# Third half tile ahead of a norm, and block making shared out anew between ScalarE and VectorE

## The reference, cut to what matters

```python
def _rmsnorm(x, g):
    y = x32 * lax.rsqrt(jnp.mean(x32 * x32, axis=-1, keepdims=True) + EPS)
    return (y * g.astype(jnp.float32)).astype(x.dtype)
def _modulate(h, shift, scale):
    return h * (1 + scale[:, None, :]) + shift[:, None, :]
...
    mod = cond @ ada_w[layer] + ada_b[layer]
    h = _modulate(_rmsnorm(x, norm1_g[layer]), sh1, sc1)
    y = _pool_mixer(...)                       # layer 0; layer 1: _dilated_attention
    hkv = _modulate(_rmsnorm(x, kv_norm_g), kv_shift, kv_scale)   # layer 1: a second activation
    kv = hkv @ w_kv
    x = x + g1[:, None, :] * y
    h = _modulate(_rmsnorm(x, norm2_g[layer]), sh2, sc2)
    x = x + g2[:, None, :] * _conv_ffn(h, w_up, conv_w, conv_b, w_down)
```

## Time and profile before

| | us |
|---|---|
| median of 3 runs | 2740.91 |
| lowest, highest | 2738.64, 2741.95 |
| the profiled execution | 2740.4 |
| its span | 2738.6 |
| PE busy in it | 2668.8 |
| DVE, ACT, POOL busy | 1391.9, 1034.7, 110.1 |

### The profile page before, as it was taken

One profiled execution on the slowest core, in us unless ns is written; L12 is line 12 of the kernel. 1 busy time (PEld: TensorE's weight loads), 2 busy tenths in 40 slices (PEclk: granted clock), 3 DMA queues, 4 the chain that ended last, 5 costly groups with the idle time before them and its releaser, 6 DMA issues.

```text
span 2738.6 us, 32934 instructions
## 1 busy us (share of the span) xinstructions
PE 2668.8 (97%) x13810; PEld 2148.9 (78%) x13810; DVE 1391.9 (51%) x2147; ACT 1034.7 (38%) x1525; POOL 110.1 (4%) x87
## 2 busy tenths in 40 slices
PE   7989999999999999999999999999999999999998
PEld 3578888877777777888888777788888777788887
DVE  6767767544444445543445654543444554543343
ACT  2243233453333334532343554422233555432232
POOL 0000000000000000000000110010010110010010
PEclk9989999999999999999999999999999999999999
DMA  7445645322222121223223121223223121223232
GB/s 299 185 161 207 247 180 204 116 82 78 78 78 72 68 78 62 78 98 110 93 94 121 50 81 55 101 94 105 92 97 118 62 77 62 92 93 115 78 104 74
DMA packets 46850, 297.03 MB, mean 108 GB/s; under 512 B 5104, under 2 KB 7280, under 8 KB 17520
## 3 DMA queue, kind: packets, MB, share of 16 engines
q1 hardware_dynamic: 46560, 294.42, 29.5%
q10 hardware_dynamic: 144, 0.52, 0.1%
HBM read 292.82 MB, written 2.10 MB: 108 GB/s over the span
## 4 chain that ended last, share of the span: by engine, by line
PE 90%; ACT 2%; DVE 2%; issue 0%; DVEq 0%
PE PS L506 88%; PE PS L564 1%; DVE WL L1414 1%; ACT H1H L972 0%; ACT WH L972 0%; DVE AR L1437 0%; DVE XT L1417 0%; DVE AA L1414 0%; ACT H2Hb L972 0%; ACT V0b L972 0%; ACT V1b L972 0%; DVE H1L L1414 0%; ACT AA L972 0%; ACT V2b L972 0%; ACT OC L972 0%
## 5 line engine op out<-in xcount | busy, mean ns | idle before, releaser
L506 PE MATMUL PS<-H1H,WH 128*128 128x512 f32 (+1 forms) x2256 | 885.8, 393 | 20.3 <-DVE WL L1414 12.6
L506 PE MATMUL PS<-H1H,WL 128*128 128x512 f32 (+1 forms) x2256 | 865.5, 384 | 0.0
L506 PE MATMUL PS<-H1L,WH 128*128 128x512 f32 (+1 forms) x2256 | 864.8, 383 | 0.0
L1414 DVE TENSOR_TENSOR WL<-RAW,WH 128x1024 fp32r<-128x1024 f32 (+1 forms) x400 | 526.8, 1318 | 461.3 <-ACT WH L972 460.7
L972 ACT ACTIVATE WH<-RAW 128x1024 fp32r<-128x1024 f32 (+1 forms) x400 | 439.7, 1101 | 270.0 <-PE PS L506 242.8
L506 PEld LDWEIGHTS PS<-H1H,WH 128*128 128x128 f32 x2256 | 427.6, 190 | 114.0 <-DVE WL L1414 16.7
L506 PEld LDWEIGHTS PS<-H1L,WH 128*128 128x128 f32 x2256 | 427.8, 190 | 84.3 <-issue 5.5
L506 PEld LDWEIGHTS PS<-H1H,WL 128*128 128x128 f32 x2256 | 427.1, 189 | 83.0
L506 PE MATMUL PS<-H2Hb,WH 128*128 128x512 f32 (+1 forms) x408 | 162.5, 398 | 4.0 <-issue 3.0
L506 PE MATMUL PS<-H2Hb,WL 128*128 128x512 f32 (+1 forms) x408 | 155.1, 380 | 0.0
L506 PE MATMUL PS<-H2Lb,WH 128*128 128x512 f32 (+1 forms) x408 | 154.8, 380 | 0.0
(11 more groups left out here) (252 smaller groups left out, 3085.0 us busy)
## 6 DMA issues: line engine op xcount, KB each, us to landing
RAW<-stream SPq DMA_DIRECT2D x170, 1024.0 KB, 4.8
AR<-stream SPq DMA_DIRECT2D x56, 1024.0 KB, 6.9
RAW<-stream SPq DMA_DIRECT2D x64, 704.0 KB, 4.0
...
```

The source lines that it names most:

```text
L506: return nc.tensor.matmul(out, weights, moving, start=start, stop=stop, skip_group_check=True)
L1414: return nc.vector.tensor_tensor(out, a, b, op)
```

## The change

- `HALVED` gives a number of half tiles for each norm: three for norms 1 to 3, still two for the last. Tiles 14, 74 and 154 are now multiplied in halves as well. `SQN`, `SUMN`, `RES`, `nth` and `added` count accordingly. Part 0's norm stands four blocks into the first half 1, in a bank of its own.
- `banks` writes out the banks of the half tiles and of the next three tiles by hand.
- The plain block V is made by DVE (`shifted`, a `tensor_scalar` with two operations) instead of ACT; DVE runs divide, shifted and low one, two and three blocks behind each other, and residuals, sums and preps stand between them. ACT makes the high block only.
- At edge 2 ACT makes each block of the second activation's high part after that block's second high half of the first; the plain blocks follow, in six buffers instead of three.
- `entry` takes four blocks of x = 0, then four of x = 1, then the norm of part 1, then the rest.
- The prep of the last tile of the projection and one iteration of the loops ahead move into the edge. At edge 1 three modulations in a row stand ahead of it.
- At the end `final_g_2` is multiplied into x by ACT ahead of DVE's last step, which becomes a `tensor_tensor`.

The diff, cut to its core:

```diff
-HALVED = (1, 2, 3, 8)
-
-RES = {"pool": 0, FFN0: 10, WO0: 28, FFN1: 38, OUT0: 54, FFN2: 62, OUT1: 78, FFN3: 86}
+HALVED = {1: 3, 2: 3, 3: 3, 8: 2}
+
+RES = {"pool": 0, FFN0: 11, WO0: 30, FFN1: 41, OUT0: 57, FFN2: 65, OUT1: 81, FFN3: 89}
...
-    for t in range(FFN0, ATT0 - 2):
+    place(halves(14, 1, "norm1") + list(range(FFN0, FFN0 + 3)), (0, 1, 2, 3, 4, 5, 7, 6, 0, 1))
+    for t in range(FFN0 + 3, ATT0 - 3):
         take(t)
-    halves(ATT0 - 2, "norm2")
-    for t in range(ATT0, ATT0 + 3):
-        take(t, (2, 3, 4))
+    place(halves(ATT0 - 3, 2, "norm2") + list(range(ATT0, ATT0 + 3)), (5, 6, 0, 1, 5, 6, 7, 2, 3, 4))
...
         for part in range(2):
-            for x in range(2):
+            for x in range(m):
                 b = BANK[t + x, part]
                 q.wait_ge(*c.low(t + x))
                 vacate(b)
                 for k in order:
-                    if (part, x, k) == (1, 0, order[n // 2]):
+                    if (part, x, k) == (1, 0, order[4]):
                         half_norm(v, bank, 0)
...
-        for k in range(8):
-            if k == 4:
-                half_norm(v, bank, 1)
-            for x in range(2):
+        for x in range(2):
+            for k in range(4):
                 some(x, 0, k)
-        for k in range(8):
-            some(2, 0, k)
+        half_norm(v, bank, 1)
+        for x, blocks in ((0, (4,)), (1, (4,)), (2, range(5))):
+            for k in blocks:
+                some(x, 0, k)
+        for k in range(5, 8):
+            for x in range(3):
+                some(x, 0, k)
         for k in range(4):
             for x in range(3):
...
-            kw = {"scale": c.AB[:, gains + k:gains + k + 1], "bias": c.mod(shift + k, 1)}
-            q.wait_ge(c.nt, 8 + n + e + 1)
-            act(part_of(c.H1H, k, part), T, ACT.Identity, **kw)
-            q.wait_ge(c.nld, n + e - 3 if e > 3 else n)
-            act(c.NORM[v]["V"][e % 4][:, 0:256], T, ACT.Identity, **kw).then_inc(c.nv, 1)
+            q.wait_ge(c.nt, 8 + 16 * a - 16 + e + 1)
+            act(part_of(c.H1H, k, part), c.NORM[v]["T"][e % 3][:, 0:256], ACT.Identity,
+                scale=c.AB[:, gains + k:gains + k + 1], bias=c.mod(shift + k, 1)).then_inc(c.nh, 1)
         return make
 
     def edge(v, bank, first, t0, out, make):
 
+        prep(t0 - 1)
+        for k in (5, 6, 7):
+            half_square(v, k, 0, first)
+        half_root(v, bank, out, 0)
+        make(0, 0)
+        half_square(v, 5, 1, first)
+        make(0, 1)
         prep(t0)
-        half_square(v, 6, 0, first)
-        half_square(v, 7, 0, first)
-        half_root(v, bank, out, 0)
+        make(0, 2)
+        make(0, 3)
         half_square(v, 6, 1, first)
+        make(0, 4)
         prep(t0 + 1)
-        for k in range(4):
-            make(0, k)
+        make(0, 5)
         half_square(v, 7, 1, first)
+        make(0, 6)
         prep(t0 + 2)
-        make(0, 4)
-        make(0, 5)
         half_root(v, bank, out, 1)
-        make(0, 6)
         make(0, 7)
         for k in range(8):
...
 
     def for_kv(part, k):
 
-        e = 8 * part + k
-        T = part_of(c.AT, k, part)
-        kw = {"scale": c.AB[:, 24 + k:25 + k], "bias": c.mod(96 + k, 1)}
-        q.wait_ge(c.at, e + 1)
-        act(part_of(c.AH, k, part), T, ACT.Identity, **kw)
-        q.wait_ge(c.al1, e - 2)
-        act(c.AV[e % 3][:, 0:256], T, ACT.Identity, **kw).then_inc(c.av1, 1)
+        q.wait_ge(c.at, 8 * part + k + 1)
+        act(part_of(c.AH, k, part), part_of(c.AT, k, part), ACT.Identity, scale=c.AB[:, 24 + k:25 + k],
...
-        q.wait_ge(c.al1, 16)
-        q.wait_ge(c.al0, k - 2)
-        act(c.AV[k % 3][:, :], chunk(c.AT, k), ACT.Identity, **kw).then_inc(c.av0, 1)
+        q.wait_ge(c.al0, k - 5)
+        act(c.AV0[k % 6][:, :], chunk(c.AT, k), ACT.Identity, scale=c.AB[:, 16 + k:17 + k], bias=c.mod(48 + k, 1)
+            ).then_inc(c.av0, 1)
         if k in (1, 4):
             prep(ATT0 + 3 + k // 3)
...
-    half_root(8, BANK["last"], c.SG, 0)
-    half_square(8, 6, 1, last)
-    half_square(8, 7, 1, last)
-    half_root(8, BANK["last"], c.SG, 1)
+    for part in range(2):
+        for k in (6, 7):
+            half_square(8, k, part, last)
+        if part == 0:
+            q.wait_ge(c.gl, 88)
+            q.wait_ge(c.sp, 44)
+        half_root(8, BANK["last"], c.SG, part)
+        for k in (6, 7):
+            x = part_of(c.XT, k, part)
+            q.wait_ge(c.sq, SQN[8] + nth(8, k, part))
+            act(x, x, scale=c.cols("final_g_2", k)).then_inc(c.gained, 1)
 
...
-
-        prep(t0)
-        left(6, 0)
+            half_residual(first, k, t0 - 8 + k, part, gate, v)
+
+        prep(t0 - 1)
+        for k in (5, 6):
+            left(k, 0)
...
-        q.wait_ge(c.sq, SQN[v] + 7 + 2 * part)
-        q.wait_ge(c.ssum, SUMN[v] + 5)
+        for n in range(18):
+            if n < 16:
+                divide(n)
+            if 1 <= n < 17:
+                shift(n - 1)
+            if n >= 2:
+                low(n - 2)
+            if n == 0:
+                left(5, 1)
+            elif n == 2:
+                half_sum(v, 5, 1)
+                prep(t0)
+            elif n == 4:
+                left(6, 1)
+            elif n == 5:
+                half_sum(v, 6, 1)
+                prep(t0 + 1)
+            elif n == 6:
+                left(7, 1)
+            elif n == 7:
+                prep(t0 + 2)
+
+    def half_sum(v, k, part):
...
         return make
 
+    def shifted(a, v, gains, shift):
+
+        def make(e):
+            k, n = e % 8, 16 * a - 16
+            q.wait_ge(c.nt, 8 + n + e + 1)
+            q.wait_ge(c.nld, n + e - 3 if e > 3 else n)
+            nc.vector.tensor_scalar(c.NORM[v]["V"][e % 4][:, 0:256], c.NORM[v]["T"][e % 3][:, 0:256],
+                                    c.AB[:, gains + k:gains + k + 1], c.mod(shift + k, 1), ALU.mult, ALU.add
+                                    ).then_inc(c.nv, 1)
...
     modulation()
     modulation()
-    for n in range(6):
+    for n in range(5):
         prep(11 + n)
         q.wait_ge(c.ada, 12)
         residual(RES["pool"], n, 9 + n, 16)
         add_square(1, n)
         modulation()
+    modulation()
     modulation()
...
-        q.wait_ge(c.res, RES[FFN3] + 16 + 2 * part)
+        q.wait_ge(c.res, RES[FFN3] + 8 + nth(8, 7, part))
         for k in range(8):
             x = part_of(c.XT, k, part)
-            stt(x, x, c.cols("final_g_2", k), part_of(c.SG, 0, part), ALU.mult, ALU.mult).then_inc(c.yd, 1)
+            q.wait_ge(c.gained, nth(8, k, part) if k >= 6 else k + 1)
+            tt(x, x, part_of(c.SG, 0, part), ALU.mult).then_inc(c.yd, 1)
 
```

More of the change, by code:

```diff
@@ L220, in banks @@
         take(t, (0, 1, 4))
-    for t in range(WO0 + 3, FFN1 - 2):
+    for t in range(WO0 + 3, FFN1 - 3):
         take(t, (2, 3, 5, 6, 7))
-    halves(FFN1 - 2, "norm3")
-    for t in range(FFN1, IN0):
+    place(halves(FFN1 - 3, 3, "norm3") + list(range(FFN1, FFN1 + 3)), (0, 1, 2, 3, 4, 5, 7, 6, 0, 1))
+    for t in range(FFN1 + 3, IN0):
         take(t)
@@ L234, in banks @@
             take(t)
-    halves(NTILE - 2, "last")
+    place(halves(NTILE - 2, 8, "last"), (0, 1, 2, 3, 7))
     return of
@@ L600, in halves @@
                 ins.then_inc(c.mm if part else c.half, 1)
-                free[b] = (c.res, first + 7 + 2 * part + x)
+                free[b] = (c.res, first + nth(v, 8 - m + x, part))
     def entry(t0, H, L, ready, v, bank, freed):
@@ L692, in ffn @@
             last = {0: (2, "norm2"), 3: (8, "last")}.get(f) if half else None
-            for n in range(6 if last else 8):
+            for n in range(8 - HALVED[last[0]] if last else 8):
                 gemm(t0 + 30 * half + 22 + n, c.GH[f], c.GL[f], lambda k: (c.gl, 22 * f + HC * half + k + 1),
@@ L814, in pe_program @@
     group(WO0, [(c.H1H, c.H1L, ho)] * 3, [(c.res, RES[WO0] + n + 1) for n in range(3)], split=7, hook=tail)
-    for n in range(3, 6):
+    for n in range(3, 5):
         gemm(WO0 + n, c.H1H, c.H1L, ho, (c.res, RES[WO0] + n + 1))
-    halves(WO0 + 6, c.H1H, c.H1L, 3, BANK["norm3"], RES[WO0])
+    halves(WO0 + 5, c.H1H, c.H1L, 3, BANK["norm3"], RES[WO0])
     ffn(1, FFN1, None, (3, BANK["norm3"]))
@@ L1132, in ffn @@
                 table("natural_log_exp")
-            for n in range(6 if half and f in (0, 3) else 8):
+            for n in range({0: 5, 3: 6}.get(f, 8) if half else 8):
                 prep(t0 + 30 * half + 24 + n)
```

147 lines of the change are left out of this document (74 added, 73 removed).

## The result

The changed kernel takes 2723.3 us (median of four runs, 2721.7 to 2725.0) against 2741.4 (2738.6 to 2744.6) of the kernel before in the same rounds: ratio 0.9934, 95% interval 0.9916 to 0.9951, 18.1 us faster. 2722.9 was predicted, from 2716 to 2732.

A forecast was written before the change was run, and what follows sets the result against it. TensorE, busy 2668.8 of 2738.6 us, sets the pace, so only its gaps at three edges can be bought back. Gains 5.1 + 10.9 + 1.7 + 0.3 = 18.0 from 2740.9 give 2722.9 us, range 2716 to 2732.

The forecast's parts named there:

- Edge 1: Tiles 15 to 19, a projection's end normalised before the next matrix: ends at 182.1 instead of 187.2, gain 5.1 us.
- The slow stretch: At tiles 15 to 19: matmuls at half clock after the 2.7 us wait for WL 19, costing 1.7 us.
- Edge 2: Tiles 75 to 81: entry ends 551.9 instead of 556.27, gain 4.4; with the VF wait gone too, 10.9 us in all.
- the 2.96 us of the bank: Tile 77 waits for bank 2, where tile 76's second half stood; moved to bank 6, the wait and slow stretch go.
- Edge 3: Tiles 155 to 159: PE waits 1.7 for WL 158 and 1.4 for WL 159, ends 1134.5 instead of 1136.2, gain 1.7 us.
- TENSOR_SCALAR: DVE's plain-block instruction at the edges: taken at 0.27 us apart, making 0.95 us per block against ACT's 0.98 before.
- The end: Last step: SP's output DMA issues set the end, so only 0.07 and some 0.2 us count, gain 0.3 us.
- some 0.2 of an earlier residual: At the kernel's last step: an earlier residual on DVE saves some 0.2 us of the 0.3 gained there.
- B: Rival: VectorE becomes the bound, TENSOR_SCALAR at 0.40 or more, slow stretches at all edges; gain 11, 2730; 0.25 together with E.
- C: Rival: no slow stretch at edge 1 and WL waits shorter than worked out; gain 23 us, 2718; chance 0.15.
- D: Rival: two waits per entry keep the clock low through all three entries; 21 us slower, 2762; chance 0.05.
- E: Rival at edge 2: ACT's 1.2 us per block push VF behind PE by up to 4 us; gain 11, 2730; 0.25 with B.

## Why the prediction was right, and where its steps were off

**Edge 1 (predicted 5.1, measured 5.9).** By its steps: PE at tile 16 at 142.4; 141.62 + 1.0 for the earlier start = 142.6. Norm 0 at 149.3; 149.6. WL 18 and 19 let PE go at 160.9 and 166.7; 161.4 and 167.3. The waits were put at 1.9 and 2.7 and are 0.29 + 1.54 and 1.07. The slow stretch was put behind the last wait; it came behind the one before it, and since it made PE late for WL 19, it used up part of that wait and cost little. The run with two halves at edge 3, which is the same program here, shows the other order, the one predicted (PE):

```profile
159.14 0.39 PE L523 MATMUL PS<-H1H,WH 128*128 128x256 f32 x1 [1.54 <-DVE WL L1438]
...
160.68 0.59 PE L523 MATMUL PS<-SS,ONES 128*128 128x256 f32 x2
...
165.07 0.39 PE L523 MATMUL PS<-H1H,WH 128*128 128x256 f32 x1 [2.66 <-DVE WL L1438]
...
166.22 0.42 PE L523 MATMUL PS<-H1L,WH 128*128 128x256 f32 x1
```

There the wait of 1.54 left the clock up (norm in 0.59), 2.66 us of waiting followed and then the slow stretch, which then counts in full: this execution passed norm 0 1.2 us ahead of the changed kernel's and left the edge 0.25 behind it. From tile 15's wait on, edge 1 gave 5.4 us in this execution, 5.9 in the changed kernel's and 6.3 in that with the second activation back, of the same program here: what 5.1 fell short by is of the size of this chance. One reading in 5.1 was off as well: the end of before, 187.2, was taken from a WH that starts 0.2 us behind PE's own row (187.03), with which it is 4.9.

**Edge 2 (10.9, measured 11.2).** The bank and the interleaving, which frees VF, are each shown by its own undoing: 3.4 and 5.6 us at the place. Entry 4.4, measured 4.15; VF's copy at 558.5 less the 6.9 us of distance is 551.6, measured 551.25. The wait for the third WL: 1.4, measured 1.27. One argument of the prediction did not hold: that the 2.96 us of the bank were a saving by themselves. They were one only together with the earlier blocks.

**Edge 3 (1.7, measured 1.5).** Waits of 1.7 and 1.4, measured 1.54 and 1.27, with 0.29 ahead of them that was left out. The end of the entry was put at 1134.5; with the distance just ahead of the edge it is 1116.72 + 17.79 = 1134.5. The 0.2 missing is the end of before, again read off a WH 0.2 us behind PE's own row.

**TENSOR_SCALAR.** Taken at 0.27 apart, it was 0.32 (0.41 long). That is the mis-sized term: 0.05 us in each of 16 blocks. It moved the low blocks by tenths, and the run with one operation (0.26 apart) shows that 0.2 to 0.26 us of it reach the end of an edge. The prediction had read in the Trainium skill ("VectorE: DVE Perf Modes", section on mode 2x_2P) that an fp32 operation with one tensor source in SBUF makes two elements a cycle. With one operation the row here is indeed shorter, 354 ns against 418 of the two-tensor form; with two operations and two columns it takes 413 ns, and nothing of that is left to see.

**The end (0.3, measured 0.57).** SP's issues do set the very last us, as said. What was mis-sized is the "some 0.2 of an earlier residual": it is 0.5, for that residual stands behind all eight multiplications of part 0.

**What was not foreseen** is the 1.1 us at tile 349. The prediction read the banks at edge 2, where a stall was, and not the rest of the table that the same edit renumbers. The predicted places gave 5.9 + 11.2 + 1.5 + 0.6 = 19.2 us instead of 18.0; tile 349 and the clock ahead of edge 3 took 1.5 away and the early start added 1.0. That the sum came as near as 0.7 us in the profiled execution and 0.4 us in the median is in part luck; that the waits went, and where, is not.

**The rivals.** B needed TENSOR_SCALAR at 0.40 apart or more and slow stretches at all edges: it was 0.32, and one of three had a stretch. The argument against B, that gaps under 1.8 us at edge 3 have no slow stretch behind them, does not hold: the 1.75 us ahead of edge 3 had one, and so had 1.54 at edge 1. C was half there: the slow stretch at edge 1 came, and the waits for WL were 6.7 us in all instead of the 9.1 worked out. D (slow through the entries) did not happen; the longest stretch within an entry was 3.3 us. E did not happen at ScalarE's 1.2 us per block; at the 1.69 of the run with its plain blocks PE waits, though for low blocks and not for VF.
